# Moving half of the conditioning products of a projection stage from TensorE to VectorE

## The reference, cut to what matters

```
mod_ctx = einsum('bd,de->be', silu(c_ctx), w_mod) + b_mod
mod_lat = einsum('bd,de->be', silu(c), w_mod) + b_mod
...
sh1, sc1, g1, sh2, sc2, g2 = split(mod, 6)
h = rmsnorm(x, norm1_g) * (1 + sc1) + sh1
p = einsum('bnd,de->bne', h, w_in)          # 2048 -> 4608, the projection
...                                          # rope, two kinds of attention
x = x + g1 * einsum('bne,ed->bnd', o, w_out)
h2 = rmsnorm(x, norm2_g) * (1 + sc2) + sh2
x = x + g2 * ec_moe(h2, ...)                 # 16 experts
```

## Time and profile before

| | |
|---|---|
| median of 3 runs | 2361.98 us (2360.32 to 2363.41) |
| span of the profiled execution | 2364.1 us, from its first to its last instruction |
| TensorE busy | 2215.2 us, 94% |
| VectorE busy | 1512.7 us, 64% |
| ScalarE busy | 1202.5 us, 51% |
| mean granted TensorE clock | 0.970 |

### The profile page before, as it was taken

How to read it: one execution, slowest core, us unless ns; L and a number is a source line. 1 busy time by engine, 2 the same in 40 slices (tenths; PEclk the granted TensorE clock), 3 DMA queues, 4 the chain that set the end, 5 groups by cost and what they waited for, 6 DMA issues and landing times.

```text
span 2364.1 us, 28774 instructions
## 1 busy us (share of the span) xinstructions
PE 2215.2 (94%) x10944; PEld 1547.9 (65%) x10944; DVE 1512.7 (64%) x1577; ACT 1202.5 (51%) x1255; POOL 241.9 (10%) x97
## 2 busy tenths in 40 slices
PE   5899999999999997999929999999999999999993
PEld 3467777777877775788826666666666666666662
DVE  3242221233556665333268999999999999999994
ACT  4431221122246666112147777777776777777763
POOL 1010000001000000000000111211122222111211
PEclk8999999999999997999959999999999999999997
DMA  9875566654220003222389999999999999999995
GB/s 371 317 238 213 221 235 240 232 196 179 72 92 1 1 1 139 95 72 70 127 318 363 382 383 382 395 390 388 389 388 386 385 382 394 395 386 387 384 376 189
DMA packets 187519, 623.71 MB, mean 264 GB/s; under 512 B 10960, under 2 KB 12496, under 8 KB 156048
## 3 DMA queue, kind: packets, MB, share of 16 engines
q1 hardware_dynamic: 177328, 565.76, 63.0%
q0 software_dynamic: 6112, 35.40, 5.4%
q10 hardware_dynamic: 4000, 21.50, 2.3%
HBM read 593.08 MB, written 29.56 MB: 263 GB/s over the span
## 4 chain that ended last, share of the span: by engine, by line
PE 88%; DMA 5%; DVE 3%; ACT 1%; SPq 1%; issue 1%; POOL 0%; ACTq 0%; POOLq 0%; DVEq 0%
PE ps L560 25%; PE ps L561 24%; PE ps L562 24%; PE ps L809 3%; PE ps L755 3%; PE ps L843 3%; DMA arena<-in_w_mod 2%; PE ps L826 1%; PE ps L830 1%; PE ps L958 1%; DVE mx L1545 1%; DMA xn_d<-arena 1%; SPq L624 1%; PE ps L896 1%; PE ps L786 1%
## 5 line engine op out<-in xcount | busy, mean ns | idle before, releaser
L1748 DVE TENSOR_TENSOR E_w_lo<-arena,E_w_hi 128x2048 fp32r<-128x2048 f32 x384 | 871.2, 2286 | 88.5 <-ACT E_w_hi L1248 79.4
L1248 ACT ACTIVATE E_w_hi<-arena 128x2048 fp32r<-128x2048 f32 x380 | 728.8, 1918 | 277.0 <-PE ps L562 277.0
L560 PE MATMUL ps<-E_w_hi,E_xsT_hi 128*80 128x512 f32 x1024 | 404.6, 395 | 2.3 <-DVE E_xsT_lo L1741 2.3
L561 PE MATMUL ps<-E_w_hi,E_xsT_lo 128*80 128x512 f32 x1024 | 403.1, 394 | 0.0
L562 PE MATMUL ps<-E_w_lo,E_xsT_hi 128*80 128x512 f32 x1024 | 400.2, 391 | 0.0
L1528 DVE TENSOR_TENSOR B_w_lo<-arena,B_w_hi 128x1024 fp32r<-128x1024 f32 x72 | 87.6, 1224 | 369.3 <-ACT B_w_hi L1076 369.0
L560 PE MATMUL ps<-B_w_hi,B_x_hi 128*128 128x512 f32 x720 | 290.5, 403 | 1.6 <-DVE B_x_lo L1532 1.1
L561 PE MATMUL ps<-B_w_hi,B_x_lo 128*128 128x512 f32 x720 | 282.2, 392 | 0.0
L562 PE MATMUL ps<-B_w_lo,B_x_hi 128*128 128x512 f32 x720 | 281.7, 391 | 0.0
L1076 ACT ACTIVATE B_w_hi<-arena 128x1024 fp32r<-128x1024 f32 x72 | 75.6, 1058 | 338.9 <-DMA arena<-in_w_in 293.0
L1360 POOL DMA_INDIRECT acc_d<-arena,idxC x16 | 148.9, 9309 | 765.1 <-DVE arena L1792 765.1
(11 more groups left out here) (202 smaller groups left out, 2548.2 us busy)
## 6 DMA issues: line engine op xcount, KB each, us to landing
arena<-in_w_expert_gate SPq DMA_DIRECT2D x128, 1024.0 KB, 12.9
arena<-in_w_expert_up SPq DMA_DIRECT2D x128, 1024.0 KB, 12.5
arena<-in_w_expert_down SPq DMA_DIRECT2D x128, 1024.0 KB, 15.2
arena<-in_w_mod SPq DMA_DIRECT2D x64, 1024.0 KB, 6.4
arena<-in_w_in SPq DMA_DIRECT2D x36, 1024.0 KB, 5.0
arena<-in_w_mod SPq DMA_DIRECT2D x64, 512.0 KB, 9.7
arena<-in_w_out SPq DMA_DIRECT2D x16, 1024.0 KB, 5.3
acc_d<-arena POOLq DMA_DIRECT2D x1, 5120.0 KB, 30.2
```

What stands on the lines that cost most here:

```text
L560: eng.matmul(out, x_hi, w_hi, start=start, stop=False)
L561: eng.matmul(out, x_lo, w_hi, start=False, stop=False)
L1248: act.activation(split_e(j)[0][:, :], at(slot_e(j), D), ACT.Copy).then_inc(xw_hi, 1)
L1748: dve.tensor_tensor(w_lo[:, :], at(slot_e(j), D), w_hi[:, :].bitcast(F32), ALU.subtract).then_inc(xw_lo, 1)
```

## The change

Of the 64 chunks the first 32 (n=32 to 63, groups 2 and 3) are no longer multiplied on TensorE. A new step `mac` does one chunk on VectorE: for each of the two conditioning vectors one instruction over 128x2048 that multiplies the chunk with the vector's 128 numbers, one for each partition, and adds it to a running sum `macs` (for the first chunk of a group it only multiplies). After 16 chunks a new step `macsum` on TensorE sums over the partitions: eight matmuls whose weights `pick` are a column of ones and zeros. The buffer of `macs` lies where q is put later.

`MACS_AT` places the `mac` steps, all at odd k: two in o=0, six in o=1, eight in o=2, seven in o=3, eight in o=4, one in o=5. The other 32 chunks stay on TensorE as 16 pairs; `PAIRS_AT` now places them two k apart (before: three), in o=5, o=6 and o=7. Loads still go by `LOADS`; chunk n+2 now waits for `mac` of n. Within a step of k the `mac` stands before the `split`.

```diff
-PAIRS_AT = [()] + [(1, 4, 7, 10, 13)] * 6 + [(1, 4), ()]
+N_MAC = 2 * KC
+N_PAIRED = N_MODA + N_MAC
+MACS_AT = [(13, 15), (3, 5, 7, 9, 11, 13), tuple(range(1, 16, 2)), tuple(range(3, 16, 2)), tuple(range(1, 16, 2)), (1,)]     + [()] * 3
+PAIRS_AT = [()] * 5 + [(5, 7, 9, 11, 13, 15), (1, 3, 5, 7, 9, 11, 13), (0, 2, 4), ()]
...
+            if k in MACS_AT[o]:
+                steps.append(("mac", c))
+                c += 1
+                if c % KC == 0:
+                    mi = group_of(c - 1)
+                    later.append((3, ("macsum", mi)))
+                    later.append((3, ("modcopy", mi)))
...
-    free = {s: i for i, s in enumerate(STEPS)}
+    free = {("mod", s[1]) if s[0] == "mac" else s: i for i, s in enumerate(STEPS)}
...
+        macs = at(Q0, 2, D)
...
+                elif kind == "macsum":
+                    mi = step[1]
+                    pe.wait_ge(mod_copied, mi)
+                    pe.wait_ge(pick_ready, 2)
+                    for v in range(2):
+                        pe.wait_ge(mac_done[v], KC * (mi - 3))
+                    for v in range(2):
+                        for c in range(4):
+                            mm = pe.matmul(bank(5)[32 * c:32 * (c + 1), :], pick[:, v, :], macs[:, v, NB * c:NB * (c + 1)],
+                                           start=(v == 0), stop=(v == 1), skip_group_check=True)
+                    mm.then_inc(mod_done, 1)
...
+            def conditioning_sum(n):
+
+                where, s, fill = mod_slot(n)
+                i, k = n - N_MODA, n % KC
+                dve.wait_ge(mod_landed[s], 16 * fill)
...
+                for v in range(2):
+                    if k == 0:
+                        ins = dve.tensor_scalar(macs[:, v, :], at(where, D), cT[:, k, v:v + 1], None, ALU.mult)
+                    else:
+                        dve.wait_ge(mac_done[v], i)
+                        ins = dve.scalar_tensor_tensor(out=macs[:, v, :], in0=at(where, D), scalar=cT[:, k, v:v + 1],
+                                                       in1=macs[:, v, :], op0=ALU.mult, op1=ALU.add)
+                    ins.then_inc(mac_done[v], 1)
```

More of the change, by code:

```diff
@@ L81 @@
 N_MODA = 2 * KC
-PAIRS_AT = [()] + [(1, 4, 7, 10, 13)] * 6 + [(1, 4), ()]
-assert 2 * sum(map(len, PAIRS_AT)) == 4 * KC
+N_MAC = 2 * KC
+N_PAIRED = N_MODA + N_MAC
+MACS_AT = [(13, 15), (3, 5, 7, 9, 11, 13), tuple(range(1, 16, 2)), tuple(range(3, 16, 2)), tuple(range(1, 16, 2)), (1,)]     + [()] * 3
+PAIRS_AT = [()] * 5 + [(5, 7, 9, 11, 13, 15), (1, 3, 5, 7, 9, 11, 13), (0, 2, 4), ()]
+assert sum(map(len, MACS_AT)) == N_MAC and 2 * sum(map(len, PAIRS_AT)) == 4 * KC - N_MAC
 UNITS = NT * HEADS
@@ L120, in make_steps @@
         steps += [("xsplit", 4 * q + i) for i in range(4)]
-    n, later = N_MODA, []
+    n, later, c = N_PAIRED, [], N_MODA
     for o, b in enumerate(ORDER):
@@ L129, in make_steps @@
             later = [x for x in later if x[0] > 0]
+            if k in MACS_AT[o]:
[5 more added lines that the diff above has]
+                    later.append((3, ("modcopy", mi)))
+                    if GROUPS[mi] in (3, 4):
+                        later.append((5, ("cols", mi)))
             if k in PAIRS_AT[o]:
@@ L153, in make_steps @@
                     steps.append(("shape", ORDER[o - 1], k // 2))
-    assert n == 6 * KC and not later
+    assert n == 6 * KC and c == N_PAIRED and not later
     return steps
@@ L276, in build @@
         grows = at(H0 + RING_A * SLOT + 1792, P)[0:33, :]
+        macs = at(Q0, 2, D)
+        assert 2 * D <= DH * TOK
         qT = at(Q0, HEADS, TOK)
@@ L326, in build @@
         ctmp = sb("ctmp", [P, 32])
+        pick = sb("pick", [P, 2, 32])
         modT = sb("modT", [P, 6, 2, KC])
@@ L375, in build @@
         mod_done = sem("mod_done")
+        mac_done = [sem(f"mac_done{v}") for v in range(2)]
+        pick_ready = sem("pick_ready")
         mod_copied = sem("mod_copied")
@@ L521, in after_mod @@
             g, (k, size) = group_of(n), place_in_group(n)
-            if k == size - 1:
+            if N_MODA <= n < N_PAIRED:
+                for v in range(2):
+                    eng.wait_ge(mac_done[v], n - N_MODA + 1)
+            elif k == size - 1:
                 eng.wait_ge(mod_done, g + 1)
             else:
-                eng.wait_ge(mod_used, n - g + 1)
+                eng.wait_ge(mod_used, n - g + 1 - (0 if n < N_MODA else N_MAC - N_MAC // KC))
         def after_products(eng, o, k):
@@ L1390, in _ @@
             dve.memset(cT[:, :, :], 0.0).then_inc(cT_zero, 1)
+            dve.memset(pick[:, :, :], 0.0).then_inc(pick_ready, 1)
             def mean_squares(b):
@@ L1450, in fold_gains @@
                             link(dve.tensor_tensor(so[:, :, h, :], si[:, :, h, :], gsw[:, :, 1 - h, :], ALU.mult))
+            def conditioning_sum(n):
+                where, s, fill = mod_slot(n)
+                i, k = n - N_MODA, n % KC
+                dve.wait_ge(mod_landed[s], 16 * fill)
+                if i == 0:
+                    dve.wait_ge(xn_ready, NT)
+                    dve.wait_ge(xp_done, transposes_before(("x", NT - 1, 3)) + 1)
+                    after_mod(dve, N_MODA - 1)
+                elif k == 0:
+                    dve.wait_ge(mod_done, group_of(n))
+                for v in range(2):
+                    if k == 0:
[5 more added lines that the diff above has]
+                    ins.then_inc(mac_done[v], 1)
             for step in STEPS:
                 kind = step[0]
-                if kind == "cvec":
+                if kind == "mac":
+                    conditioning_sum(step[1])
+                    if step[1] == N_MODA:
+                        dve.wait_ge(pick_ready, 1)
+                        for v in range(2):
+                            ins = dve.memset(pick[:, v, v:v + 1], 1.0)
+                        ins.then_inc(pick_ready, 1)
+                elif kind == "cvec":
                     b = take(0)
```

## The result

The changed kernel takes 2371.25 us (median of 5 runs, 2368.24 to 2372.52), the kernel before in the same series 2361.98 us (5 runs, 2360.17 to 2363.41). The medians are 9.3 us apart. The ratio is 1.0033, with a 95% interval of 1.0022 to 1.0045: slower by 0.2 to 0.5%. The forecast was 2343 us, 0.8% faster.

A forecast was written before the change was run, and what follows sets the result against it. The prediction took TensorE, busy 94%, as the bound. Pairs removed -33.9, `macsum` +4.2, stalls +10, pair refills +0.5 gave -19.2 us: 2343 us from 2361.98, range 2336 to 2350 us with chance 0.56.

The forecast's parts named there:

- What TensorE is relieved of: TensorE in the projection: 16 pairs go, 33.9 us off, two `macsum` add 4.2 us, net 29.7 us less.
- A `mac`'s price: VectorE: one chunk of two accumulating instructions costs 4.55 us, from a 2351 ns trace row; 141 us in all.
- Does VectorE have the room?: VectorE in o=1 and o=2: full before any wait, with 56.7 us of work in 55.6 and 54 in 56.7.
- The loop: Load cycle in the backlog: `mac`, refill, weight chunk, ScalarE and VectorE split; 14.2 us for 4 k against TensorE's 13.6 to 14.5.
- the stretch step by step: Table of VectorE's end times against TensorE's needs from o=1 on: stalls of 6.2 us in o=1, 3.6 in o=2.
- about 10 us, which I keep: Sum of TensorE's stalls for late splits in o=1 to o=4, entered in the forecast as 10 us.
- signs of being wrong: Stalls over 2 us in o=3 and o=4, line 775 waiting for `in_w_mod` in o=5 and o=6, accumulations far from 2.35 us.
- the table: Step-by-step list for o=1 of when VectorE ends and TensorE wants each split: single stalls of 0 to 1.8 us.
- In o=3 seven `mac` and in o=4 no shaping: After o=2, VectorE is let off and its splits run ahead by 0 to 5 us: no stall in o=3 or o=4.
- Late by 0 to 0.3 us: Remaining pairs, two k apart in the second half: refills late by this much per gap, 0.5 us for 13 gaps.
- The second rival: The load cycle holds through o=3 and o=4 too: stalls of 16 to 25 us, 2350 to 2358 us; chance 0.17.
- The rival with slower pairs: Remaining pairs outrun their loads, 6.8 us apart instead of 10.2: 2364 us, up to 2375; chance 0.08.

The follow-up runs named there:

- e9_short_macs: Changed kernel with weight chunks loaded ahead of `mac` refills, pairs' refills ahead of weight chunks, and every `mac` on 64 of 2048 columns: 2335.71 us, ratio 0.9871.
- e1_chunk_first: Changed kernel with only SyncE's load order altered: weight chunks go ahead of the refill waiting for the `mac` at k=1, 5, 9, 13; 2338.56 us, ratio 0.9890.

## Why the prediction was wrong

**What TensorE is relieved of** was right: 29.7 us forecast, 29.0 measured between the block sums of the kernel before and e9_short_macs. **A `mac`'s price** was right, 4.61 us against 4.55, and so was the choice of the row it was taken from: 2345 ns for the accumulating form with two float32 operands from SBUF. By the rule of the Trainium skill ("Vector Engine (DVE) Microarchitecture Reference", Points that are easy to get wrong) the throughput should have been half; the trace of the changed kernel disagrees, with 60 instructions at 2345 ns where plain TENSOR_TENSOR of this size takes 2286. **"Does VectorE have the room?"** asked a question that mattered for about one us. It has room.

**The loop** was described in the prediction, link by link, with 14.2 us (14.56 measured; the sum of its terms 7.25, 0.1, 1.06 and 1.14 is 9.55 and not 9.65, so 14.1). What failed is the step "the stretch step by step" and its sum of "about 10 us, which I keep". It was mis-sized, 10.5 us with the second half against 33, and the difference turned the sign. Two of the prediction's own signs of being wrong came: over 2 us lost in o=4, and line 775 waiting for `in_w_mod` (2.6 us in all on TensorE). What was missing:

- At the starts of o=2 and o=3 the table let TensorE go when the low part was ready. It also waits for ScalarE's copy, which stands behind two splits: 3.8 and 3.9 us. And the chunk in question landed 8.66 us after its issue, where I had 7.25 after its refill's. o=1 and o=2 lost 19.2 us instead of 9.8.
- "In o=3 seven `mac` and in o=4 no shaping: ahead by 0 to 5 us, no stall." In o=3 this held (0.3 us). In o=4 it contradicted the loop as costed: 14.2 is above 13.6, and the lead is used up. 3.9 us.
- After the last `mac` I had no term at all. Its lag went into o=5: weight chunk, ScalarE's split, and behind that split ScalarE's copy of the finished group, for which the first pair waits 4.2 us. With the low clock behind it o=5 lost 6.7 us. The chain of the changed kernel there (the pair takes 2.66 us instead of 1.9):

```profile
415.32 7.77 DMA arena<-in_w_in
423.30 0.83 issue
424.14 0.59 ACT arena L1100
424.77 2.66 PE ps L775 x16
```

- "Late by 0 to 0.3 us" for the pairs' refills: 2.9 us in o=6 instead of 0.5: in the chain there the refills landed 8.1 to 9.4 us after their pair.
- TensorE's products all stood at 0.227 us, with no term for the clock. It fell behind the three long waits, and that is 5 of the 33 us.

**The second rival** (the loop holds through o=3 and o=4, 16 to 25 us) had the right mechanism, with a chance of 0.17 and still too small a price, though o=3 itself lost only 0.3 us. It should have been the forecast. Its price was taken from the loop's surplus over TensorE alone, 1 to 2 us a chunk, and not from the other work that queues behind the late link on ScalarE. The rival with slower pairs had its sign right and its place wrong: it accounts for 3 of 33 us.

What stays open: the changed kernel's runs scatter over 4.3 us, and of its 9.3 us the profiled pair shows 4.1 in the stage. The profiled execution was the fastest, with a mean granted clock of 0.969 over the whole run; the other four have 0.965 to 0.968, and 0.001 of 2370 us is 2.4 us. So more time at the low clock may be the rest, but they have no trace, and it isn't shown.

## What to carry to other kernels

When work moves to an engine whose result frees a buffer, look at the queue that refills it before the engine's spare time. An in-order queue ties whatever stands behind that refill to the new engine, and here four such links in each block cost 34 us together, where the moved work itself cost about one. Follow each link until it closes: a loop of load, split, moved work and next load has a length, and if it is longer than the bound engine's time for the same step it sets the pace, at any busy share. Then add what stands behind the late link on every engine in it, at block ends above all, and what TensorE's clock does behind a long wait.

## What was not expected of the hardware

Weight chunks of one size and form don't all land equally fast. In the kernel before, the issues at 201.31 and 217.56 us (median us to landing of one):

```profile
arena<-in_w_in SPq DMA_DIRECT2D x1, 1024.0 KB, 6.2
arena<-in_w_in SPq DMA_DIRECT2D x1, 1024.0 KB, 5.0
```

There the one for k=0 to 3 of the next block is always late, 5.7 to 6.5 us four times, where most others take 4.8 to 5.0. The one at 201.31 us went out 3.8 us after the last refill of the pair at k=10 (197.5 us, landed 7.2 us later), so the two flights overlap; the last refill before 217.56 us went out at 210.3 us and landed 6.5 us later, so there they don't. That isn't enough for the changed kernel. There three took 8.4 to 8.7 us, at 202.81, 266.36 and 341.55 us, and most others 7.0 to 7.3, those for k=0 to 3 of o=4 and o=5 among them (7.2). The one at 341.55 us serves k=4 to 7 of o=4 and flies beside the five stores of `dv_d` (337.75 to 342.12 us); its counterparts beside such stores took 6.5 us in the kernel before and in e1_chunk_first. The one at 202.81 us flies beside a store of `out` (204.58 us). For the one at 266.36 us the views show nothing of the kind. These are overlaps in time, and no run took one away, so the cause isn't shown.
